# Down projection of a feed-forward block by Strassen's scheme, and a new order of its tiles, on one core

## What is computed

```python
D_MODEL, SEQ, D_FF = 1024, 512, 3 * 1024
h = rms_norm(x, norm2_g[l])
u = causal_dwconv(jnp.einsum('bsd,df->bsf', h, w_up[l]), ffn_conv_w[l])   # width 3, 2 * D_FF channels
gate, up = jnp.split(u, 2, axis=-1)
x = x + jnp.einsum('bsf,fd->bsd', jax.nn.gelu(gate) * up, w_down[l])
...
return rms_norm(x, final_g)
```

## Time and profile before

| | |
|---|---|
| median of 3 runs | 1285.92 us (1284.54 to 1286.01) |
| the profiled execution | 1285.49 us, span 1283.0 us |
| mean granted TensorE clock | 0.997 |
| busy: PE / PEld | 1267.4 us / 931.6 us |
| busy: DVE / ACT / POOL | 673.6 / 474.4 / 456.5 us |
| read from HBM | 221.86 MB |

### The profile page before, as it was taken

How to read it: one execution, slowest core, us unless ns; L and a number is a source line. 1 busy time by engine, 2 the same in 40 slices (tenths; PEclk the granted TensorE clock), 3 DMA queues, 4 the chain that set the end, 5 groups by cost and what they waited for, 6 DMA issues and landing times.

```text
span 1283.0 us, 15358 instructions
## 1 busy us (share of the span) xinstructions
PE 1267.4 (99%) x6128; PEld 931.6 (73%) x6128; DVE 673.6 (52%) x1180; ACT 474.4 (37%) x645; POOL 456.5 (36%) x218
## 2 busy tenths in 40 slices
PE   8999999999999999999999999999999999999998
PEld 5789888766687444444376788888888888888887
DVE  2487996877854443323268548322642541541553
ACT  4353334466433211112157733432431431431443
POOL 3154457177430000000143153444453444444440
PEclk9999999999998999999999999999999999999999
DMA  9535584001157899999941130322232222223101
GB/s 373 236 126 186 201 342 179 33 34 66 66 220 284 337 427 426 427 426 427 427 187 66 66 131 33 131 99 99 73 125 99 98 92 105 76 92 127 66 1 66
DMA packets 33906, 226.98 MB, mean 177 GB/s; under 512 B 3888, under 2 KB 4528, under 8 KB 7856
## 3 DMA queue, kind: packets, MB, share of 16 engines
q1 hardware_dynamic: 31104, 216.63, 43.3%
q10 hardware_dynamic: 1584, 5.24, 1.1%
q0 software_dynamic: 1152, 4.19, 0.9%
HBM read 221.86 MB, written 4.19 MB: 176 GB/s over the span
## 4 chain that ended last, share of the span: by engine, by line
PE 95%; DVE 2%; DMA 1%; ACT 1%; issue 0%; POOL 0%; SPq 0%; DVEq 0%
PE psum L1019 24%; PE psum L1020 23%; PE psum L1021 23%; PE psum L1575 13%; PE psum L1345 2%; PE psum L1310 1%; DVE x L2690 1%; DMA x<-in_x 1%; PE psum L1660 1%; PE psum L1535 1%; PE psum L1560 1%; PE psum L1563 0%; PE psum L1038 0%; PE psum L1068 0%; PE psum L1454 0%
## 5 line engine op out<-in xcount | busy, mean ns | idle before, releaser
L938 POOL TENSOR_TENSOR w_lo<-raw,w_hi 128x1024 fp32r<-128x1024 f32 x79 | 192.2, 2433 | 539.2 <-ACT w_hi L1864 533.3
L1019 PE MATMUL psum<-b_hi,w_hi 128*128 128x512 f32 x608 | 238.2, 392 | 0.1
L1021 PE MATMUL psum<-b_hi,w_lo 128*128 128x512 f32 x608 | 236.7, 389 | 0.0
L1020 PE MATMUL psum<-b_lo,w_hi 128*128 128x512 f32 x608 | 236.6, 389 | 0.0
L942 POOL TENSOR_TENSOR w_lo<-raw,w_hi 128x1024 fp32r<-128x1024 f32 x79 | 198.1, 2508 | 0.0
L1864 ACT ACTIVATE w_hi<-raw 128x2048 fp32r<-128x2048 f32 (+1 forms) x80 | 151.8, 1898 | 111.5 <-PE psum L1021 91.4
L1019 PEld LDWEIGHTS psum<-b_hi,w_hi 128*128 128x128 f32 x608 | 114.1, 188 | 30.7 <-issue 5.7
L1021 PEld LDWEIGHTS psum<-b_hi,w_lo 128*128 128x128 f32 x608 | 114.1, 188 | 23.9
L1020 PEld LDWEIGHTS psum<-b_lo,w_hi 128*128 128x128 f32 x608 | 114.2, 188 | 23.4
L1575 PE MATMUL psum<-ex_ring,xe 128*64 128x512 f32 x432 | 95.0, 594 | 0.0
L2688 DVE TENSOR_TENSOR x<-psum,x 128x512 f32<-128x512 f32 x39 | 26.9, 692 | 127.6 <-PE psum L1021 127.6
(11 more groups left out here) (479 smaller groups left out, 2254.9 us busy)
## 6 DMA issues: line engine op xcount, KB each, us to landing
raw<-in_stream SPq DMA_DIRECT2D x97, 1024.0 KB, 4.9
ex_ring<-in_stream SPq DMA_DIRECT2D x78, 1024.0 KB, 19.8
ex_more<-in_stream SPq DMA_DIRECT2D x18, 1024.0 KB, 20.9
mod_in<-in_stream SPq DMA_DIRECT2D x8, 1024.0 KB, 20.1
x<-in_x SPq DMA_DIRECT2D x4, 512.0 KB, 6.4
x<-in_x ACTq DMA_DIRECT2D x1, 2048.0 KB, 7.5
xt<-h2t ACTq DMA_DIRECT2D x8, 256.0 KB, 9.6
out<-y_out SPq DMA_DIRECT2D x4, 512.0 KB, 2.9
```

Of the source, the lines that this page charges most:

```text
L938: nc.gpsimd.tensor_tensor(w_lo[:, slot, w], raw[:, raw_slot, w], w_hi[:, slot, w].bitcast(F32), ALU.subtract)
L1019: mm(o, w[0], x[0], start=start, stop=False)
L1020: mm(o, w[0], x[1], start=False, stop=False)
L1021: return mm(o, w[1], x[0], start=False, stop=stop)
```

## The change

In quarters 0 to 2 the down projection of a pair of output blocks (256 channels) is a product of 2 x 2 blocks: weights of 128 channels out by 384 in, and inputs of 384 channels by 256 tokens. It is done with seven block products in place of eight (`PRODUCTS`, `OUT_OF`). For that, VectorE makes four sums of inputs per block of three (`first_term`, `terms`, and their low parts in `low_terms`) and four sums of weights per pair (`weight_sum`), and adds each product to its quarter of `x1` (`add_part`). Products go to banks 4 and 5 by pair, where several are accumulated one on the other, and to 6 and 7; the intermediate sum is read from the bank after each. The up tiles use banks 0 to 3. The first pair of up tiles of the next quarter comes ahead of the products. Weights are split in steps of 1024 columns (up tiles) or 384 (the 28 weight forms of a quarter) in a ring of 48 blocks. The last quarter keeps its eight down tiles. The hardware loop is gone.

```diff
+def product_order():
+    first = [(0, 1), (0, 2), (0, 5), (0, 6), (1, 1), (0, 3), (0, 7), (1, 5), (0, 4)]
+    for p in range(1, FPAIRS - 1):
+        first += [(p, 6), (p, 3), (p + 1, 1), (p, 7), (p, 2), (p + 1, 5), (p, 4)]
+    return first + [(FPAIRS - 1, n) for n in (6, 3, 7, 2, 4)]
+OUT_OF = {1: (0, 0), 2: (0, 0), 5: (1, 1), 6: (0, 1), 7: (1, 1), 3: (0, 1), 4: (1, 0)}
+TERM = {5: 0, 6: 1, 7: 2, 4: 3}
+SUM_OF = {5: 1, 7: 2, 6: 3, 3: 4}
...
-    p.phase(5)
+    p.phase(4)
+    def up_tiles(q, i):
+        g = q * FQ + i
+        p.add("ff_g", q, i, by=("accg_done", g + 1), bank=2 * g % 4)
+        p.add("ff_u", q, i, by=("accu_done", g + 1), bank=2 * g % 4 + 1)
+    up_tiles(0, 0)
+    for q in range(SEVEN):
+        for i in range(1, FQ):
+            up_tiles(q, i)
+        up_tiles(q + 1, 0)
+        for pair, n in PRODUCTS:
+            p.add("part", q, pair, n, by=("part_done", part_count(q, pair, n)),
+                  bank={2: 7, 5: 6, 3: 6}.get(n, 4 + pair % 2))
+    for i in range(1, FQ):
+        up_tiles(SEVEN, i)
+    for j in range(KD):
+        p.add("ff_o", SEVEN, j, by=("resid_done", RES_LAST + j + 1), bank=(2, 3, 4, 0, 1, 2, 3, 4)[j])
...
+            def part(q, p, n):
+                o = open_tile("part", q, p, n)
+                o = o[:, 0:FH]
+                w = step_weights("form", q, p, n)
+                if n in (2, 3):
+                    pe.wait_ge(lo_done, SPLITS["ff", q, FQ - 1] + 1)
+                for k in range(FK):
+                    if n == 1:
+                        pe.wait_ge(lo_done, SPLITS["ff", q, k] + 1)
+                        x = ffx(k, low)
+                    elif n in (2, 3):
+                        x = ffx(FK + k, low if n == 2 else high)
+                    else:
+                        pe.wait_ge(t_lo_done, q * FK + k + 1)
+                        x = t_hi[:, k, TERM[n], :], t_lo[:, k, TERM[n], :]
+                    last = mm3(o, block_of(w, k), x, k == 0 and n in (1, 2, 5), k == FK - 1, n in (6, 7, 3, 4))
+                done(last)
+            def last_down(last_half):
+                q = SEVEN
+                o2 = open_tile("ff_o", q, 0), open_tile("ff_o", q, 1)
+                for k in range(FQ):
+                    pe.wait_ge(lo_done, SPLITS["ff", q, k] + 1)
+                    for i in range(2):
+                        last = mm3(o2[i], down_block(i, k), ffx(k, slice(0, T)), k == 0, k == FQ - 1)
...
+            for q in range(SEVEN):
+                for i in range(2 if q == 0 else 1, FQ):
+                    up_pair(q, i)
+                up_pair(q + 1, 0)
+                for p, n in PRODUCTS:
+                    part(q, p, n)
+            for i in range(1, FQ):
+                up_pair(SEVEN, i)
...
+            for q in range(QUARTERS):                       # on VectorE
+                for i in range(0 if q == 0 else 1, FQ):
+                    for half in range(2):
+                        factor(half, q, i)
+                        taps(half, q, i, True, True)
+                    gated(q, i)
+                    if i >= 1:
+                        low_of(q, i - 1)
+                    if q < SEVEN:
+                        if i == 1:
+                            first_term(q, 0)
+                        if 1 <= i < FK:
+                            first_term(q, i)
+                        if i >= FK:
+                            terms(q, i - FK)
+                        if i > FK:
+                            low_terms(q, i - FK - 1)
+                        if i in (FK, FK + 1):
+                            weight_sums(q, i - FK)
+                low_of(q, FQ - 1)
+                if q == SEVEN:
+                    continue
+                factor(0, q + 1, 0)
+                taps(0, q + 1, 0, True, True)
+                low_terms(q, FK - 1)
+                factor(1, q + 1, 0)
+                for i, (p, m) in enumerate(PRODUCTS):
+                    add_part(q, p, m)
+                    if i == 0:
+                        taps(1, q + 1, 0, True, False)
+                    if i == 1:
+                        taps(1, q + 1, 0, False, True)
+                    if i == 2:
+                        gated(q + 1, 0)
+                    if 3 <= i < 7:
+                        weight_sum(q, 2, tuple(SUM_OF)[i - 3])
+                    if 10 <= i < 14:
+                        weight_sum(q, 3, tuple(SUM_OF)[i - 10])
```

More of the change, by code:

```diff
@@ L966, in add_probs @@
                         .then_inc(psum_done, 1)
-            for c in range(1, NSPLIT):
+            for c in range(1, FFN_FIRST):
                 if SPLIT0["wo"] <= c <= SPLIT0["wo"] + NHL:
@@ L1833, in last_half @@
                     half_columns(0)
-            quarter(QUARTERS - 1, last_half=last_half)
+            last_down(last_half)
             for n in (1, 3, 4):
@@ new lines, in factor, with taps @@
+            def factor(half, q, i):
+                o = take(("ff_g", "ff_u")[half], q, i)
+                V.tensor_tensor(o, o, rstd, ALU.mult).then_inc(ffz_done, 1)
+            def taps(half, q, i, first, last):
+                g = q * FQ + i
+                a = (acc_g, acc_u)[half][:, g % 2, :]
+                o = bank(("ff_g", "ff_u")[half], q, i)
+                tap = lambda k: cols[:, cw + half * 3 * FF + k * FF + g:cw + half * 3 * FF + k * FF + g + 1]
+                if first:
+                    dve.wait_ge(acc_done, 2 * g + half + 1)
+                    link(V.scalar_tensor_tensor(out=a[:, 1:T], in0=o[:, 0:T - 1], scalar=tap(1), in1=a[:, 1:T],
+                                                op0=ALU.mult, op1=ALU.add))
+                if last:
+                    V.scalar_tensor_tensor(out=a[:, 2:T], in0=o[:, 0:T - 2], scalar=tap(0), in1=a[:, 2:T],
+                                           op0=ALU.mult, op1=ALU.add).then_inc((accg_done, accu_done)[half], 1)
@@ new lines, in weight_sums, with add_part @@
+            def weight_sums(q, p):
+                for n in SUM_OF:
+                    weight_sum(q, p, n)
+            added_to = {}
+            def add_part(q, p, n):
+                o = take("part", q, p, n)
+                o = o[:, 0:FH]
+                row, half = OUT_OF[n]
+                dst = x1[:, 2 * p + row, half * FH:(half + 1) * FH]
+                if (p, row, half) in added_to:
+                    dve.wait_ge(part_done, added_to[p, row, half])
+                V.tensor_tensor(dst, o, dst, ALU.add).then_inc(part_done, 1)
+                added_to[p, row, half] = part_count(q, p, n)
```

405 lines of the change are left out of this document (262 added, 143 removed).

## The result

| | before | after |
|---|---|---|
| median of 5 runs each, same chip | 1286.01 us (1284.54 to 1288.17) | 1291.65 us (1290.81 to 1292.87) |
| profiled execution / its span | 1285.49 / 1283.0 us | 1290.81 / 1288.6 us |

The ratio of the times is 1.0045, interval 1.003 to 1.0059: slower, where 0.3% faster had been forecast. The time lies above the range of 1279 to 1287.

The account below looks back on a forecast made before the run. TensorE, busy 99% of the span, was taken to bound the kernel. From the profiled 1285.49 us, -7.2 (products) and +3.3 (bank stop) gave 1281.6; from the runs' median, 1282.0 us, 8-in-10 range 1279.0 to 1287.0.

Parts of the forecast that it names:

- Products, -7.2: Down products of three quarters: 252 matmuls of 256 columns at 0.1200 us replace 144 of 512, saving 7.2 us in all.
- the rival that their pace is worse: In the 252 product matmuls, many waits and weight loads slow the pace; at 0.13 us each, 1289.6 us; chance 0.08.
- Order of the up tiles, 0: Next quarter's first two up tiles moved ahead of the products: nothing added, 10.88 us of cover for the last operands.
- Bank stop, +3.3: Ahead of the last quarter's down tiles, TensorE stands still once until the last up tile's taps free bank 3: 3.3 us.
- The clock in that stop: Rival: the clock halves at the stop ahead of the last down tiles, costing 1.7 to 3.5 us; chance 0.18.
- ScalarE and GpSimd, cover: Weight forms for the products are made before they are wanted, GpSimd's work being 57 us of a 95.5 us quarter: cost 0.
- Cost taken: 0; bounds 0 and 1 us a quarter: Around the products, VectorE makes operands and frees banks in time: cost 0, at most 1 us a quarter.
- 384 columns take 0.55 and 1024 take 1.22: VectorE's operation times in us, read from widths 256 and 512; bounds 0.42 to 0.69 for 384 columns.
- the walk: VectorE's operations summed from the sixth pair's end into the products: 7.52 us against 10.88, first addition ending 1.7 us in.
- a slack of 0.46 us: Tightest margin for VectorE's addition where only one product lies between two on the same bank, four times a quarter.
- VectorE is late for the banks: Rival: VectorE operations 0.15 us dearer make additions late in the products, 4.8 us in all, 1286.8 us; chance 0.10.
- 1278.7: Rival's time in us: no stop ahead of the last down tiles because their banks come free earlier; chance 0.08.

Follow-up runs that it names:

- narrow low parts: The kernel after with GpSimd's low part of each of the 84 weight forms cut from 384 to 128 columns, output not exact: 1284.63 us.
- a sixth place: The kernel after with the third weight sum of a pair written into unused columns of its own chunk, so five buffers serve two sums a pair: 1287.25 us.

## Why the prediction was wrong

- **Products, -7.2: right.** The short steps have a mean of 0.1199, and where VectorE keeps up a stretch is 30.23 or 30.24 against 30.24 forecast. The rival that their pace is worse is refuted. The 109.2 ns that the Trainium skill's formula gives ("TensorE: Matmul & The Clock Gate", Back-to-back issue gap) are not seen: what rows of the same width had shown held.
- **Order of the up tiles, 0: right.** The table above closes without a term for it.
- **Bank stop, +3.3: right** in place, cause and size (3.52 from start to start less 0.23), and shown by taking it out.
- **The clock in that stop: open in the prediction, and open in the runs.** In the profiled execution of the kernel after the rival did not come true: the granted clock is 1.00 all through the stop and behind it, and so with narrow low parts. In the other three executions with the same stop it did, at the lower end of the 1.7 to 3.5 us that the prediction gave it: 3.4 us at half speed, 1.6 to 1.7 us. The Trainium skill ("TensorE: Matmul & The Clock Gate", Why this matters for your kernels) would have it fall in all five; three agree and two don't. Nothing here shows what parts them, nor in which of the kernel after's four other executions it fell.
- **The clock inside the products** was in no rival. In the first product stretch of the kernel after, behind two stops, steps of 1.59 and 0.59 us, the granted clock is 0.50 from 965 to 966 and 16 matmuls from 964 to 967.3 start 0.21 apart, 1.5 us in all. As the run with a sixth place shows, it took the place of waits for VectorE and added nothing. No other execution had the fall there, though one had steps of 1.04 and 0.59 us at this place.
- **ScalarE and GpSimd, cover: right as to their own work.** No wait of TensorE on a weight form is in the waits of this stage. But GpSimd was held to cost nothing because it was early, and it set VectorE's pace.
- **VectorE, "Cost taken: 0; bounds 0 and 1 us a quarter": the step that failed.** It measured 3.94, 1.44 and 2.29 us, each over the upper bound. VectorE came too late with two things, the additions that free the banks and, at the first stop of the first and third quarters, the last `t_lo`. Inside the step, three readings were wrong. First, "384 columns take 0.55 and 1024 take 1.22" by a line through two other widths: correct beside an idle GpSimd, up to 1.36 and 2.07 beside a busy one. The bound of 0.69 for 384 columns was made from widths alone and could not hold this. Second, the walk looked at banks and operands and left out the wait ahead of the sixth intermediate sum, 0.90 us in each quarter; without it 2.9 of the 7.67 us are gone. Third, a slack of 0.46 us, four times a quarter, was called enough for a walk with a dozen interpolated prices in it. "VectorE is late for the banks" was the rival that came true, given a chance of 0.10, for the fuller stretch named there, but at 7.7 us and not 4.8. That the fuller stretch would be the cause was right; why its operations cost more, GpSimd beside them and a missing buffer, stood nowhere in the prediction.
- **The sum.** The profiled execution's span is 1288.6 us against the forecast 1279.1. Of these 9.5, 7.67 are the stops inside the products and 1.72 is where the block began; that goes with the granted clock between 400 and 430 us (0.83 in place of 0.89, 1.7 us), ahead of anything changed. The medians lie 9.65 apart (1282.0, 1291.65), and only one execution of the five has a trace.
- **The range.** Its lower end, 1279.0, is called half of the way from the forecast to 1278.7; half of the way would be 1280.4. Nothing hangs on it here, since the time came out above.
- What stays open: why the clock stays low for a different time from run to run between 402 and 426 us, what decides whether it falls behind the stop of 3.3 us, which of VectorE and GpSimd gets ahead when both start within 0.03 us, and how much of the first quarter's last 1.72 us could be had. VectorE starts that quarter behind, because the norm comes late, and its last `t_lo` beside GpSimd lasts 2.09 there.

## What to carry to other kernels

Price a VectorE operation by its operands' places and by what GpSimd does at that moment, not by its width alone. Look for rows of the same operation that are twice as long as the rest; here such a row ends when GpSimd's running operation ends plus the operation's own time, less 0.13 us. Where a schedule leaves slack of less than one operation between an addition and the next use of its bank, list every wait ahead of it, intermediate buffers as well as banks, and count the saving only after that. And when a saving vanishes, put the steps between matmuls into short ones and long ones: the short ones said at once that the scheme worked, the long ones who ate it. Where one trace a kernel is all there is, look for rows of unchanged code that came out differently before a difference is put down to the edit: one `t_lo` was worth 0.85 us here, as much as some of the edits.

## What was not expected of the hardware

- Two operands in SBUF: 384 columns 0.55 us alone and up to 1.36 beside GpSimd, 1024 columns 1.22 and up to 2.09; with one operand in PSUM nothing changes (71 additions at 0.42). The long ones end 0.13 to 0.14 us before GpSimd's running operation's end plus their own time.
- Either side can be the one that waits. GpSimd's form of 384 columns takes 1.01 to 1.04 us in the 39 rows of the kernel after that have no VectorE operation on two SBUF operands beside them, and up to 2.11 in the other 45 (mean 1.26).
- A scaling of 128 x 128 with one tensor operand took 0.28 us in the kernel before, 1.04 beside GpSimd ahead of the products, and 0.31 where it was moved to, although GpSimd works there too. These rows don't settle what it costs beside GpSimd.
- Behind the same stop of 3.3 us the granted clock fell to 0.50 in three executions of five. It fell in one behind steps of 1.59 and 0.59 us, and stayed behind steps of 1.04 and 0.59 at the same place in another kernel.
